# Where the queries' tile order is made, five or seven slots for the context weights, and the order of copies and stores at the seams of the projection

## The reference

```python
h = rmsnorm(x, rms_g) * (1 + scale) + shift
q, k, v, z_a, glu, z_b, gates = jnp.split(h @ w_in + b_in, PROJ_SPLITS, axis=-1)
y_a = attend(q, k, v) * jax.nn.silu(z_a)
y_b = conv_branch(glu, dw_w, dw_b, ln_g, ln_b) * jax.nn.silu(z_b)
g_a, g_b = jnp.split(jax.nn.sigmoid(gates), 2, axis=-1)
m = g_a * (y_a @ w_proj_a) + g_b * (y_b @ w_proj_b)
return x + gate * (m @ w_out), k, v
```

## Time and profile before

| | |
|---|---|
| three runs | 1753.9, 1754.56, 1754.79 us; median 1754.56 |
| profiled execution | 1754.56 us, of which 1752.8 is the span shown by the trace |
| busy: PE, PE weight load | 1715.0 us (98%), 1452.0 (83%) |
| busy: DVE, ACT, POOL | 1200.4 (68%), 824.3 (47%), 591.8 (34%) |
| chain that ended last | PE 86%, DMA 5%, DVE 3% |
| granted clock of TensorE, mean | 0.997 |
| DMA | 282 MB, mean 161 GB/s |

### The profile page before, as it was taken

The page is one execution under the profiler, slowest core; times in us unless marked ns, Lnnn a source line. Parts: engine busy times, 40 slices in busy tenths (PEclk is TensorE's granted clock), DMA queues, the critical chain, the costliest instruction groups (busy, mean ns, idle before and its releaser), DMA issues.

```text
span 1752.8 us, 27391 instructions
## 1 busy us (share of the span) xinstructions
PE 1715.0 (98%) x9931; PEld 1452.0 (83%) x9931; DVE 1200.4 (68%) x1731; ACT 824.3 (47%) x1433; POOL 591.8 (34%) x478
## 2 busy tenths in 40 slices
PE   6999999999999999999999999999999999999998
PEld 3787888888899988878888878889888888888887
DVE  3785888788666757877687847777777655644444
ACT  3553444454576644444454437777777222312221
POOL 0044666554200037855565543322314000000000
PEclk9999999999999999999999999999999999999999
DMA  9443544324598625434333378986766676644421
GB/s 327 117 153 118 142 133 128 96 85 132 187 323 243 185 84 166 135 100 108 127 103 99 124 185 212 234 207 161 194 153 188 219 252 204 200 167 144 144 96 60
DMA packets 271753, 282.01 MB, mean 161 GB/s; under 512 B 49048, under 2 KB 218884, under 8 KB 268421
## 3 DMA queue, kind: packets, MB, share of 16 engines
q1 hardware_dynamic: 270258, 272.04, 51.9%
q10 hardware_dynamic: 1363, 8.24, 2.1%
HBM read 198.91 MB, written 81.30 MB: 160 GB/s over the span
## 4 chain that ended last, share of the span: by engine, by line
PE 86%; DMA 5%; DVE 3%; issue 2%; ACT 2%; POOL 2%; SPq 1%; POOLq 0%; DVEq 0%; ACTq 0%
PE banks L1798 37%; PE banks L2345 5%; PE banks L2899 4%; PE banks L2898 4%; PE banks L2900 4%; PE banks L2861 4%; PE banks L2863 4%; PE banks L2862 4%; DMA w_raw<-in_w_in 3%; PE banks L2311 2%; PE banks L1928 2%; PE banks L1927 2%; PE banks L1926 2%; PE banks L2317 2%; PE banks L2286 1%
## 5 line engine op out<-in xcount | busy, mean ns | idle before, releaser
L1798 PE MATMUL banks<-a_hi,w_hi 128*128 128x512 f32 x1176 | 461.0, 392 | 1.1 <-DVE w_lo L1410 0.5
L1798 PE MATMUL banks<-a_hi,w_lo 128*128 128x512 f32 x1176 | 458.4, 390 | 0.0
L1798 PE MATMUL banks<-a_lo,w_hi 128*128 128x512 f32 x1176 | 458.4, 390 | 0.0
L1491 DVE SCALAR_TENSOR_TENSOR banks<-glu_out,taps,banks 128x1009 f32<-128x1009 f32 (+1 forms) x240 | 342.2, 1426 | 5.3
L1798 PEld LDWEIGHTS banks<-a_hi,w_hi 128*128 128x128 f32 x1176 | 221.1, 188 | 50.9 <-issue 4.1
L1798 PEld LDWEIGHTS banks<-a_hi,w_lo 128*128 128x128 f32 x1176 | 221.2, 188 | 46.6
L1798 PEld LDWEIGHTS banks<-a_lo,w_hi 128*128 128x128 f32 x1176 | 221.2, 188 | 45.2
L1005 POOL TENSOR_TENSOR t_raw<-w_raw 128x512 f32<-128x512 f32 x39 | 54.0, 1385 | 395.3 <-DMA w_raw<-in_w_in 388.4
L1410 DVE SCALAR_TENSOR_TENSOR w_lo<-w_raw,w_hi 128x1024 fp32r<-128x1024 f32 x84 | 111.9, 1332 | 109.2 <-ACT w_hi L1095 107.9
L959 POOL TENSOR_TENSOR w_lo<-t_raw,w_hi 128x1024 fp32r<-128x1024 f32 x70 | 171.8, 2462 | 27.4 <-ACT w_hi L1095 25.2
L2454 ACT ACTIVATE probs<-scores,stat 128x640 f32<-128x640 f32 (+2 forms) x128 | 106.7, 834 | 52.8 <-DVE stat L2381 51.2
(11 more groups left out here) (229 smaller groups left out, 3428.4 us busy)
## 6 DMA issues: line engine op xcount, KB each, us to landing
w_raw<-in_w_in SPq DMA_DIRECT2D x34, 1024.0 KB, 5.6
cw_raw<-in_w_in SPq DMA_DIRECT2D x44, 512.0 KB, 5.1
proj<-out_stage SPq DMA_DIRECT2D x80, 256.0 KB, 2.2
gates_in<-proj SPq DMA_DIRECT2D x64, 256.0 KB, 3.0
q_split<-q_rows SPq DMA_DIRECT2D x8, 1152.0 KB, 5.6
w_ada<-in_w_ada SPq DMA_DIRECT2D x8, 1024.0 KB, 10.9
w_raw<-in_w_in SPq DMA_DIRECT2D x16, 512.0 KB, 4.7
q_rows<-out_stage_r SPq DMA_DIRECT2D x64, 128.0 KB, 2.4
```

The source lines that it names most:

```text
L1491: op = dve.scalar_tensor_tensor(dst, src, by, dst, ALU.mult, ALU.add)
L1798: op = pe.matmul(out, x[w][:, b, k], y, start=(start and k == j == 0), stop=(k == H - 1 and j == 2), skip_group_check=not start)
```

## The change

The patterns of `tile_order` leave the copies and sums of q and are applied to the moving operand of its matmuls. Blocks 0 to 36 of the context stage use slots 0 to 4 in a ring, blocks 37 to 43 the slots 5, 6, 3, 0, 5, 6, 3; their loads are issued at listed blocks. C22 of the last pair goes to `stg` slot 0 instead of 6, and its copy waits for the store of C11. In pairs 0 and 20 ACT does `second_part` after two casts of the next pair's weights; in pair 20 DVE does `sum_11` after `low(21, 0)`. `conv_copy(3)` and `store_conv(3)` move from pair 19 into the context stage (blocks 2 and 6), `conv_copy(7)` and `store_conv(7)` behind copies and stores of pairs 40 and 41. Loads, squares and normalizes of chunk 3's x come some blocks earlier.

```diff
-SLOT_OF_BLOCK = [(0, 5, 6, 1, 2, 3, 4)[n % 7] for n in range(36)] + [5, 6, 1, 2, 0, 4, 3, 5]
+RING_UNTIL = 37
+SLOT_OF_BLOCK = [n % 5 if n < RING_UNTIL else (5, 6, 3, 0)[(n - RING_UNTIL) % 4] for n in range(NB)]
...
     if q == LAST_B and part in ("C21", "C22"):
-        return 5 if part == "C21" else 6
+        return 5 if part == "C21" else 0
...
-        if q == LAST_B and part in ("C21", "C22"):
-            wait_hi_read(eng, pl.last_hi[c_slot(q, part)])
+        if q == LAST_B and part == "C22":
+            eng.wait_ge(out_d[0], pl.stored[q, "C11"])
+            return
...
         if q == NQ1:
-            sp.wait_ge(mm, CU0 + BLOCK_UNIT[LAST_USE[0]] + 1)
+            sp.wait_ge(mm, CU0 + BLOCK_UNIT[40] + 1)
...
         store_part(sp, q - 1, "C21")
-        store_conv(sp, 3)
         store_part(sp, q, "C11")
+        store_part(sp, q - 1, "C12")
         load_block(sp, 1)
         load_block(sp, 2)
-        store_part(sp, q - 1, "C12")
         load_block(sp, 3)
         load_x(sp, 2, 0)
+        store_part(sp, q, "C22")
         load_block(sp, 4)
-        load_block(sp, 5)
-        store_part(sp, q, "C22")
-        load_block(sp, 6)
         load_x(sp, 2, 2)
...
-                for m in LOAD_AFTER[n]:
-                    load_block(sp, m)
-                if n in (5, 7):
-                    load_x(sp, 3, n - 5)
-                if n == LAST_USE[0]:
+                if n < RING_UNTIL - 5:
+                    load_block(sp, n + 5)
+                if n in (3, 5):
+                    load_x(sp, 3, n - 3)
+                if n == 6:
+                    store_conv(sp, 3)
+                if n in (20, 21):
+                    load_block(sp, RING_UNTIL + n - 20)
+                if n in (33, 35, 37, 38, 39):
+                    load_block(sp, {33: 39, 35: 40, 37: 41, 38: 42, 39: 43}[n])
+                if n == 40:
                     load_pair(sp, NQ1)
...
         load_first(sp, 3)
-        store_conv(sp, 7)
         store_part(sp, a, "C22")
...
         store_part(sp, b, "C12")
+        store_conv(sp, 7)
...
-            act.activation(part_ap(q, "C11"), result_ap(q, banks[:, q % 2]), ACT.Identity, bias=bias_of(kind, cols[0])).then_inc(copied, 1)
+            act.activation(slot_ap(q, "C11"), banks[:, q % 2], ACT.Identity, bias=bias_of(kind, cols[0])).then_inc(copied, 1)
...
                 first_part(q)
-            if q == NQ1:
-                second_part(q)
             high(q + 1, 0)
-            if q == 0:
-                second_part(q)
             if q > first:
                 finish_part(q - 1, "C22")
                 fourth_part(q - 1)
             high(q + 1, 1)
-            if q not in (0, NQ1):
-                second_part(q)
+            second_part(q)
...
         fourth_part(q - 1)
-        conv_copy(3)
         block_high(0)
...
                     block_high(n + 2)
+                if n == 2:
+                    conv_copy(3)
                 if 2 <= n < 6:
                     squares(2, n - 2)
-                if 10 <= n < 14:
-                    squares(3, n - 10)
+                if 7 <= n < 11:
+                    squares(3, n - 7)
...
         second_part(b)
-        conv_copy(7)
         third_part(a)
...
         finish_part(b, "C12")
+        conv_copy(7)
         first_exponents()
...
-            if q == NQ1:
-                sum_11(q)
             low(q + 1, 0)
-            if q != NQ1:
-                sum_11(q)
+            sum_11(q)
...
-                if 12 <= n < 16:
-                    normalize(7 + (n - 12) // 2, ((n - 12) % 2,))
+                if 10 <= n < 14:
+                    normalize(7 + (n - 10) // 2, ((n - 10) % 2,))
...
+            order = tile_order if PAIRS[q][0] == "q" else lambda ap: ap
             wait_low(pe, q, GROUP_OF[name] - 1)
             for k in range(H):
-                hi, lo = a_hi[a][:, k], a_lo[a][:, k]
+                hi, lo = order(a_hi[a][:, k]), order(a_lo[a][:, k])
```

More of the change, by code:

```diff
@@ L444, in tile_order @@
         return ap.rearrange("p (r b c) -> p b r c", r=QR, b=4)
-    def result_ap(q, bank):
-        return tile_order(bank) if PAIRS[q][0] == "q" else bank
-    def part_ap(q, part):
-        slot = stg[:, c_slot(q, part)]
-        return slot.rearrange("p (b r c) -> p b r c", r=QR, b=4) if PAIRS[q][0] == "q" else slot
     def slot_ap(q, part):
@@ L500, in wait_c_free @@
     def wait_c_free(eng, q, part):
-        if q == LAST_B and part in ("C21", "C22"):
-            wait_hi_read(eng, pl.last_hi[c_slot(q, part)])
+        if q == LAST_B and part == "C22":
+            eng.wait_ge(out_d[0], pl.stored[q, "C11"])
+            return
+        if q == LAST_B and part == "C21":
+            wait_hi_read(eng, pl.last_hi[5])
             return
@@ L999, in weight_sum @@
             elif q == NQ1:
-                eng.wait_ge(mm, CU0 + BLOCK_UNIT[max(LAST_USE[s] for s in (1, 2, 4))] + 1)
+                eng.wait_ge(mm, CU0 + BLOCK_UNIT[36] + 1)
             elif q == NQ1 + 1:
@@ L1083, in high @@
             elif q == NQ1:
-                act.wait_ge(mm, CU0 + BLOCK_UNIT[max(LAST_USE[s] for s in (1, 2, 4))] + 1)
+                act.wait_ge(mm, CU0 + BLOCK_UNIT[36] + 1)
             elif q == NQ1 + 1:
@@ L1114, in second_part @@
             act.wait_ge(mm, MM_AT["P6", q])
-            act.activation(part_ap(q, "C12"), result_ap(q, banks[:, q % 2]), ACT.Identity, bias=bias_of(kind, cols[1]), scale=-1.0).then_inc(copied, 1)
+            act.activation(slot_ap(q, "C12"), banks[:, q % 2], ACT.Identity, bias=bias_of(kind, cols[1]), scale=-1.0).then_inc(copied, 1)
         def third_part(q):
@@ L1120, in third_part @@
             act.wait_ge(mm, MM_AT["P7", q])
-            act.activation(part_ap(q, "C22"), result_ap(q, banks[:, q % 2]), ACT.Identity, bias=bias_of(kind, cols[1]), scale=-1.0).then_inc(copied, 1)
+            act.activation(slot_ap(q, "C22"), banks[:, q % 2], ACT.Identity, bias=bias_of(kind, cols[1]), scale=-1.0).then_inc(copied, 1)
         def fourth_part(q):
@@ L1126, in fourth_part @@
             act.wait_ge(mm, MM_AT["P4", q])
-            act.activation(part_ap(q, "C21"), result_ap(q, banks[:, q % 2]), func_of(kind), bias=bias_of(kind, cols[0])).then_inc(copied, 1)
+            act.activation(slot_ap(q, "C21"), banks[:, q % 2], func_of(kind), bias=bias_of(kind, cols[0])).then_inc(copied, 1)
             if kind in ("q", "k"):
@@ L1442, in sum_11 @@
             dve.wait_ge(copied, ACT_AT["s1", q])
-            dve.tensor_tensor(part_ap(q, "C11"), result_ap(q, Z), part_ap(q, "C11"), ALU.add).then_inc(summed, 1)
+            dve.tensor_tensor(slot_ap(q, "C11"), Z, slot_ap(q, "C11"), ALU.add).then_inc(summed, 1)
         def sum_12(q):
@@ L1447, in sum_12 @@
             dve.wait_ge(copied, ACT_AT["s2", q])
-            dve.tensor_tensor(part_ap(q, "C12"), result_ap(q, banks[:, 2 + q % 2]), part_ap(q, "C12"), ALU.add).then_inc(summed, 1)
+            dve.tensor_tensor(slot_ap(q, "C12"), banks[:, 2 + q % 2], slot_ap(q, "C12"), ALU.add).then_inc(summed, 1)
         def sum_22(q):
@@ L1452, in sum_22 @@
             dve.wait_ge(copied, ACT_AT["s3", q])
-            dve.tensor_tensor(part_ap(q, "C22"), result_ap(q, banks[:, 2 + q % 2]), part_ap(q, "C22"), ALU.add).then_inc(summed, 1)
+            dve.tensor_tensor(slot_ap(q, "C22"), banks[:, 2 + q % 2], slot_ap(q, "C22"), ALU.add).then_inc(summed, 1)
         def glu_second(q):
@@ L1585, in quad @@
             taps_at(q, 0)
+            low(q + 1, 0)
             if q == 0:
```

5 lines of the change are left out of this document (1 added, 4 removed).

## The result

The changed kernel takes 1776.49 us (median of four runs, 1775.22 to 1777.73), the kernel before beside it 1754.67: a ratio of 1.0126, 95% interval 1.0111 to 1.0140. It is 22 us slower. The forecast was 9 us slower, 1763.8, and the range ended at 1772. The profiled execution took 1779.69 with a span of 1777.9, which is 25.1 more than the span of before; individual executions of the changed kernel lie between 1772.9 and 1779.7.

A forecast was written before the change was run, and what follows sets the result against it. The prediction took TensorE, nearly full, to bound the kernel, so its waits are paid nearly in full. Parts 1 to 5 summed as 0 + 0.4 + 2.7 + 1.0 + 5.1 = 9.2 us on 1754.6: 1763.8, range 1757 to 1772.

The forecast's parts named there:

- The sign: Whole kernel: predicted slower, chance 0.81, against 0.14 for the same and 0.05 for faster.
- part 1: q's matmuls: stepped reads of the moving operand cost nothing, and ACT and DVE gain nothing; 0.
- part 4: Context blocks: ACT 1 to 2 us late by block 7, lengthening the wait for x's transposes; +1.0 (0 to 3).
- part 5: Projection's end: Q3(41) 3.0 late behind C11's store, first scores +3.3, low clock 1.8; together +5.1 (0.3 to 6.9).
- The bound of 7.4: q's 336 matmuls: upper end of the stepped reads' cost, 22 ns each, 7.4 us.
- the dear case: Rival at q's matmuls: stepped reads cost as the run of 32 did, +7.4 on top, 1771; chance 0.15.
- Part 2: Pair 0: P7(0) waits for ACT's copy, now behind high(1, 1); 0.4 us.
- Part 3: Pair 20: P7 waits 4.9 plus 1.8 low clock, 4.0 comes back near 761; net +2.7 (+0.9 to +4.5).
- The price of +5: Rival in the context stage: five slots starve TensorE, +5 over some 18 blocks, 1769; chance 0.08.
- the clock: Projection's end: two idle stretches of about 3.0 and 2.4 us bring the low clock once, 1.8.

The follow-up runs named there:

- g_runs: Kernel before, with the moving operand of the projection's matmuls read in eight run patterns and unbroken, in turn by pair; 1771.41 us, one execution.
- a_step: Kernel before with only q's tile order moved to the moving operand of its matmuls; 1758.10 us, ratio 1.0016.
- a_ring: Kernel before with only the context block changes (five slots, moved loads, squares, normalizes, conv_copy(3), store_conv(3)); 1759.20 us, ratio 1.0022.
- h_p20: Changed kernel with ACT's second_part(20) again ahead of the two casts, DVE's order left changed; 1771.51 us, ratio 1.0086.
- u_swap: Changed kernel with the ACT and DVE orders of pairs 0 and 20 put back; 1767.64 us, ratio 1.0069.
- u_end: Changed kernel with C22 of pair 41 back in slot 6, conv_copy(7) and store_conv(7) early again; 1769.88 us, ratio 1.0080.
- a_swap: Kernel before with only the ACT and DVE orders of pairs 0 and 20 changed; 1760.35 us, ratio 1.0028.
- h_both: Changed kernel with x's tiles 2 and 3 and cached keys loaded later, conv_copy(3) and store_conv(3) back in pair 19; 1774.21 us, ratio 1.0114.
- u_step: Changed kernel with q's tile order put back into the copies and sums of ACT and DVE; 1769.83 us, ratio 1.0083.
- g_load: Changed kernel with x's tiles 2 and 3 loaded behind block 5 and cached keys behind block 7; 1776.48 us, ratio 1.0120.

## Why the prediction was wrong

The sign was right, and so were the places of parts 2 to 5; the time lies outside the range, 4.5 us above its end. The steps that failed are two terms of the sum: part 1, put at 0, and part 4, put at 1.0. They measured 5.4 and 5.9 in the trace. The low clock of part 5 adds most of the rest.

- **Part 1** failed by its choice: "I take 0: the row of the shorter run shows no cost". It costs 4.2 at the matmuls and 0.7 to 2.6 at v's transposes. The bound of 7.4, from the row of 32, held. The choice rested on the thought that run length orders the rows; g_runs shows that it does not. I had one row with a cost and one without and no reason between them, and gave the dear case 0.15.
- **Part 2**: 0.4 forecast, 1.8 measured. ACT's share came out as 0.7. The rest is `low(1, 0)` ahead of the weight sums on DVE, which the step did not cost for pair 0 (the section on the change leaves these lines out as well): it took the start of the cast, 97.58, from before as if nothing ahead of it moved.
- **Part 3**: right in place, mechanism and size: 6.7 forecast, 7.2 measured at P7(20); 4.0 forecast to come back near 761, 4.2 measured. Some luck is in it: 1.8 of the 4.0 is a low clock that a_step and a_ring, with the same wait, do not have. And h_p20 and the leads add that the wait hangs on the lead of the weights and not on this one delay; it is gone in u_swap without it.
- **Part 4**: 1.0 (0 to 3) forecast, 5.9 measured at the place, 3.9 to 5.4 by undoing and alone. The mechanism was named (landings over 5.8 us hold ACT, the wait for x's transposes grows), the size was not, for two reasons. The landings were taken from before, 8.8 at most, though the change moves these very loads in between x, keys and stores; the longest became 11.1. And ACT's lateness was followed to the transposes only, not to the eviction that frees TensorE's bank, where the first 2.3 us and a low clock arose. The price of +5 stood among the rivals, but by another way: it was to be spread over 18 blocks, and stood in three waits and a low clock at blocks 5 to 13. The size is that of most executions and not of all: u_end has 2.0.
- **Part 5**: the chain was right to a tenth (Q3 3.0 late, forecast 3.0; landing 13.0, forecast 12.6). The two waits together grew by 3.7, for a forecast of 3.3: the second, 2.64, took the place of the wait of 2.32 for q, as worked out. The term mis-sized was the clock: "once, 1.8" for the two idle stretches; it was 2.4 behind Q3 and 1.6 behind the scores, 7.9 in all for 5.1. The 1.6 stands in a_step, a_ring and a_swap too, which do not have this part.

By the table of growth: 9.2 forecast; +4.2 and +1.2 (part 1), +1.4 (part 2), +0.3 (part 3), +4.9 (part 4), +2.8 (part 5), and 1.2 at the start of the kernel, where nothing was changed, make the 25.2 of the profiled execution. The median lies 3 lower; that execution's mean clock was 0.991, that of the four timed ones 0.993 to 0.996.

## What to carry to other kernels

When a change moves loads, take the landing from what will be queued around them, not from the rows of the old place. When an order on an engine changes, cost each line of the diff for every iteration that it touches; and follow a late engine to everything it holds, the banks it frees too. Where rows disagree on the price of a pattern and no reason between them is known, I would now put the middle of their range in the sum (here 3.7, for 4.2 measured). Where every part is a loss or nothing, the small misses all have one sign.

## What the runs showed of the hardware

- The price of a stepped moving operand is not ordered by run length: of 227 ns between starts, 16 columns at a distance of 64 cost 13 more and 4 at a distance of 16 none.
- In the 16 traces TensorE waits 1.8 us or more at 43 places between 87 and 1740 us. At 34 of them the granted clock fell to 1.2 GHz, during the wait or just behind it; at 9 it did not, among them waits of 3.20 (u_swap), 3.00 (h_both) and 2.83 (u_step), all of Q3(41). It fell nowhere else in this stretch. In the table of growth a fall cost 1.6 to 2.4 us.
- The same code differed from one profiled execution to the next: by 87 us the traces stand between 1.2 ahead of and 1.2 behind that of the kernel before, with the clock low near 25 us for 0, 3.4 or 6.8 us in this order.
- A load of 512 KB issued behind 1 MB of x, the keys and two stores landed after 11.1 us, and after 5.0 when x and the keys were issued behind it and the stores still ahead (block 5 in the changed kernel and in g_load; the medians of all block loads there are 4.9 and 5.1).
